# One buffer fewer in the weight pipeline of a fused four-layer kernel

## The chip, the cores and the metric

The kernel runs on one core of a Trainium2 chip. The metric is the time on the device in microseconds (us), lower is better. The kernel before takes 1076.88 us, the median of 3 runs (1076.03 to 1077.47).

A core has five engines that run side by side, each with its own queue of instructions in program order: PE (TensorE, the matrix multiplier), DVE (VectorE), ACT (ScalarE), POOL (GpSimd) and SP (SyncE, which here only issues DMAs). They wait for one another by semaphores.

## The reference

Four layers work on one sequence of 256 tokens with 1024 features, all in 32-bit floats. Cut to what matters:

```
x (1, 256, 1024)
layer 0: h = rms_norm(x); proj = h @ even_w_in            # 1024 x 5120
         q, k, v, z_a, u, z_b = split(proj)
         o_a = stick_breaking_attention(q, k, v) * silu(z_a)
         o_b = s5_mixer(u, ...) * silu(z_b)               # complex diagonal state space, then GLU
         x = x + concat(o_a, o_b) @ even_w_out            # 1536 x 1024
layer 1: h = rms_norm(x); proj = h @ odd_w_in             # gated linear attention
         x = x + (rms_norm(gla(q, k, v, gate)) * silu(z)) @ odd_w_out
layers 2 and 3 (w_in: 1024 x 11264):
         h = rmsnorm(x) * (1 + scale) + shift; proj = h @ w_in
         y_att = dilated_window_attention(...) * silu(za)
         y_ret = retention(...) * silu(zr)
         merged = sigmoid(ga) * (y_att @ w_proj_attn) + sigmoid(gr) * (y_ret @ w_proj_ret)
         x = x + gate * (merged @ w_out)
return rmsnorm(x, final_norm_w)
```

shift, scale and gate of layers 2 and 3 come from silu(c) @ w_ada + b_ada. Every weight matrix is used once, for all 256 tokens.

## The kernel before

**The weight pieces.** All weight matrices that meet the whole sequence are cut into 306 pieces (numbered 0 to 305 here, in the order of use): two blocks of 128 rows by up to 512 columns, 512 KB. Each large product is made of three products of numbers rounded to the format fp32r: a weight piece is split into a high part WH (the piece, rounded) and a low part WL (the piece minus WH), the activations likewise into HTh and HTl (or YTh and YTl), and PE adds high by high, low by high and high by low. So each piece passes four engines:

1. SP loads it into one of NRAW = 6 buffers RAW (`load` in `sync_program`, L2482). For piece n it first waits until DVE is done with piece n - 6, which had the buffer.
2. ACT makes WH (`hi`, L1046 through `copy`), in one of NHL = 4 buffers. It waits until the piece has landed and until PE has read piece n - 4.
3. DVE makes WL (`lo`, L1526), after ACT.
4. PE multiplies (`half`, L593 to L595 for kind N, L602, L604 and L605 for kind T, `split_half`, L631 to L633). It waits for LO, the mark of step 3. A piece has two halves, and a half is one step of the program's clock, `time`: piece n is used in steps 2n and 2n + 1. A half of kind N with 512 columns is 6 matmuls of 512 columns, a half of kind T is 12 matmuls of 256 columns.

**The order by hand.** Every engine runs a loop over `time`, and tables at the top of the program (AT_S5, AT_SB_..., AT_GLA, AT_ATT, AT_RET, ...) say at which step it does its share of the other work: attention scores, state-space tables, gates, turns of 128x128 blocks through PE, and so on. At the end of each odd step ACT and DVE do `hi` and `lo` of the piece that is AHEAD = 3 pieces further on, `hi((time + 1) // 2 + AHEAD)`. The place of such a call in an engine's queue is called a slot below. In the slot of step 2n - 7 stands piece n. All the other work of that and of earlier steps stands ahead of it in the queue.

**Where one layer gives way to the next** (`next_layer` on ACT and DVE, `open_layer` on PE), the sums of squares, the norm and the turned activations of the new layer must be made. Before them ACT and DVE handle pieces n0 + 1 to n0 + 3, where n0 is the layer's first piece (54, 90 and 198). The last three pieces of a layer ("close", kind C) and the first three of the next one are used token half by token half: first ti = 0 of all three, then ti = 1. So the second and third of them are wanted one and two steps after the first.

**At the start** pieces 0 to 3 are made ahead of the loops, and then comes the chain of small operations that makes the state-space tables of layer 0 (`s5_...`), with `s5_near` and the `head_turn` transposes of k and q (L556) on PE at steps 26 to 30.

**The memory.** `dynamic_dma_scratch_size=4096` sets the room for descriptors of the DMAs that POOL issues (L2404 to L2408, L2364 and others).

Of the kernel before, what the change touches and what calls it, by code (L numbers as in the profile page):

```python
# [14 lines left out]

P = 128
KP = 2
NRAW, NHL = 6, 4
AHEAD = 3
EPS = 1e-6  # L20
NEG = -1e30
MAGIC = 1597463007.0
# [105 lines left out]
def program(nc, t, out):  # L128
    ctx = ExitStack()
    with ctx:  # L130
# [273 lines left out]
        def raw_landed(n):  # L404
# [10 lines left out]
        pe, act, dve, pool = (Engine(e, sem(n)) for e, n in (  # L415
            (nc.tensor, "pe_step"), (nc.scalar, "act_step"), (nc.vector, "dve_step"), (nc.gpsimd, "pool_step")))
# [627 lines left out]
        def scalar_program():  # L1044
# [3 lines left out]
            def hi(n):  # L1048
                raw, wh, _ = w_in(n)
                act.wait_ge(*raw_landed(n))  # L1050
                if n >= NHL:
                    act.wait_ge(*read(n - NHL))
                copy(wh, raw).then_inc(*act.mark(HI, n))
# [34 lines left out]
            def square(l, ti, n):  # L1088

                if l < 2:  # L1090
                    act.wait_ge(*RES_V.of(l, ti, n))
                elif n == 1:
                    act.wait_ge(*RES_V.of(l, ti, "x", 1))
                else:
                    act.wait_ge(*RES_P.of(l, ti))
                i = 2 * n + ti
                nc.scalar.activation(TK[:, ti, n, :], X[:, ti, 512 * n:512 * n + 512], ACT.Square,
                                     accum_out=NSS[l + 1][:, i:i + 1]).then_inc(*act.mark(SUMSQ, l + 1, ti, n))

            def next_layer(l):  # L1100

                n0 = (0, 54, H0[0], H0[1])[l]
                square(l - 1, 0, 0)
                square(l - 1, 0, 1)
                hi(n0 + 1)
                square(l - 1, 1, 0)
                hi(n0 + 2)
                turned(l, 0, 0)
                square(l - 1, 1, 1)
                turned(l, 0, 1)  # L1110
                hi(n0 + 3)
                turned(l, 0, 2)
                turned(l, 0, 3)
                for r in range(4):
                    turned(l, 1, r)
# [257 lines left out]
            for q in range(2):  # L1373
# [1 line left out]
                    for r in range(2):  # L1375
                        turned(0, ti, 2 * q + r)
                hi(1 + q)
            hi(3)
            nc.scalar.activation(dt, co["log_dt"], ACT.Exp).then_inc(*act.mark(S5_A, "dt"))
            act.wait_ge(*S5_V.of("er"))  # L1380
            nc.scalar.activation(er, er, ACT.Exp).then_inc(*act.mark(S5_A, "er"))
# [1 line left out]
            for time in range(2 * groups["zr"]["at"] - 6):  # L1383
                if time in ENDS:
                    evac0(ENDS[time])
                if time == 1:
                    act.wait_ge(*S5_V.of("angle"))
                    nc.scalar.activation(tmp, th, ACT.Sin, scale=0.5).then_inc(*act.mark(S5_A, "half"))
                    nc.scalar.activation(sn, th, ACT.Sin).then_inc(*act.mark(S5_A, "sin"))
                if time in AT_SB_EXP:  # L1390
                    b, i = AT_SB_EXP[time]
                    act.wait_ge(*SB_W.of(b, 2 * i + 1))
                    z = flat(Z)[:, 768 * i:768 * i + 768]
                    nc.scalar.activation(z, z, ACT.Exp, scale=-1.0).then_inc(*act.mark(SB_EXP, b, i))
                if time in AT_HEAD_TURN:
                    key, c = AT_HEAD_TURN[time]
                    act.wait_ge(*side("ht", key, c))
                    if key == "k0":
                        act.wait_ge(*S5_V.of("im"))
                    dst, scale = (QT, gqs) if key[0] == "q" else (KT, co["sb_k_g"])  # L1400
                    if key[0] == "q":
                        act.wait_ge(*GQS.of("q"))
                    k = 4 * int(key[1]) + 2 * c
                    copy(dst[:, k:k + 2, :], pair(bank_of["ht", key, c]), scale=scale).then_inc(
                        *act.mark(HEAD_T, key, c))
                for b in range(2):
                    if 0 <= time - AT_SB_LN[b] < 6:
                        sb_log(b, time)
                    if time == AT_SB_VALUES[b]:
                        for ti in range(2):  # L1410
                            act.wait_ge(*side("sbo", b, ti))
                            copy(YB[b][:, ti, :], bank_of["sbo", b, ti][:, :]).then_inc(*act.mark(SB_O, b, ti))
                if time == AT_SB_VALUES[1]:
                    nc.scalar.activation(cact, co["c"], ACT.Tanh, scale=0.5).then_inc(*act.mark(CACT, "th"))
                for b, c in AT_SB_TURN.get(time, ()):
                    yt_hi(4 * b + c, "sb", b, c)
                if time in AT_S5["block"]:
                    s5_block(AT_S5["block"][time])
                if time in AT_S5["spread"]:
                    s5_spread(AT_S5["spread"].index(time))  # L1420
                if time in AT_S5["near_out"]:
                    s5_near(AT_S5["near_out"].index(time))
                if time in AT_S5["turn"]:
                    s5_turned(AT_S5["turn"].index(time))
                if time in AT_S5["out"]:
                    s5_y(AT_S5["out"].index(time))
                if time in AT_GELU.values():
                    gelu(time)
                if time in AT_GLU_OUT:
                    i = AT_GLU_OUT.index(time)  # L1430
                    act.wait_ge(*GLU_V.of(i))
                    act.wait_ge(*tile("glu", 1))
                    copy(YTh[:, 8 + 2 * i:10 + 2 * i, :], GY[:, 2 * i:2 * i + 2, :]).then_inc(
                        *act.mark(YT_HI, "glu", 2 * i))
                if time % 2:
                    hi((time + 1) // 2 + AHEAD)
# [83 lines left out]
        def vector_program():  # L1520
            vt, ts, stt = nc.vector.tensor_tensor, nc.vector.tensor_scalar, nc.vector.scalar_tensor_tensor

            def lo(n):
                raw, wh, wl = w_in(n)
                dve.wait_ge(*HI.of(n))
                vt(wl, raw, wh.bitcast(F32), ALU.subtract).then_inc(*dve.mark(LO, n))  # L1526
# [82 lines left out]
            def next_layer(l):  # L1609

                n0 = (0, 54, H0[0], H0[1])[l]
                residual(l - 1, 0, 0)
                residual(l - 1, 0, 1)
                residual(l - 1, 1, 0)
                rstd(l, 0)
                scaled(l, 0)
                residual(l - 1, 1, 1)
                lo(n0 + 1)
                turned(l, 0, 0)
                turned(l, 0, 1)  # L1620
                lo(n0 + 2)
                rstd(l, 1)
                scaled(l, 1)
                lo(n0 + 3)
                turned(l, 0, 2)
                turned(l, 0, 3)
                for r in range(4):
                    turned(l, 1, r)
# [504 lines left out]
            for q in range(2):  # L2133
# [1 line left out]
                    for r in range(2):  # L2135
                        turned(0, ti, 2 * q + r)
                lo(1 + q)
            lo(3)
            ts(gqs, co["sb_q_g"], 128.0 ** -0.5, None, ALU.mult).then_inc(*dve.mark(GQS, "q"))
            ts(gbh, co["s5_bg"], 0.5, None, ALU.mult).then_inc(*dve.mark(GB_V, "b"))  # L2140
            dve.wait_ge(*S5_A.of("dt"))
# [476 lines left out]
```

## Time and profile before

| | |
|---|---|
| median of 3 runs | 1076.88 us |
| the profiled execution | 1076.03 us |
| its span, first to last instruction | 1074.2 us |
| PE busy | 1021.6 us, 95% |
| DVE busy | 704.9 us, 66% |
| ACT busy | 565.3 us, 53% |
| POOL busy | 336.5 us, 31% |
| mean share of the 16 DMA engines, weight queue q1 | 49.6% |

Busy time is the union of an engine's instructions. PE's matmuls are pipelined, and a record ends only some tenths of a microsecond after the next one has started; the distance from start to start is what a matmul costs: 0.23 us for 512 columns, 0.12 us for 256. "Idle before, releaser" is the time for which the engine had nothing running ahead of an instruction, and what ended it. The views used below are the page of the profile, the waits (who waited for whom), the timeline (instructions in order of time, equal neighbours merged), and windows (busy time in chosen stretches, with the granted TensorE clock as a share of its full rate).

### The profile page before, as it was taken

Reading aid. Unit: us, or ns where it says so; the run is one execution under the profiler, and the core shown is the slowest. Engines: PE = TensorE matmul, PEld = TensorE weight load, DVE = VectorE, ACT = ScalarE, POOL = GpSimd, SP = SyncE. Lnnn points to the kernel's source line nnn. Section 1 sums busy time; section 2 is a strip of 40 time slices with the busy share of each in tenths; the row PEclk is TensorE's granted clock in tenths of the full one; section 3 lists DMA queues with packets and bytes.
Section 4 is the critical chain, followed back from the end, with each engine's and each line's share of the span. In section 5 each row is a group of like instructions: output and inputs, shape, how many; then the busy total and the mean of one; then the engine's idle time right before and its main releaser. Section 6 shows DMA issues by size and latency. Waiting matters only on the chain.

```text
span 1074.2 us, 15495 instructions
## 1 busy us (share of the span) xinstructions
PE 1021.6 (95%) x6084; PEld 900.2 (84%) x6084; DVE 704.9 (66%) x1072; ACT 565.3 (53%) x872; POOL 336.5 (31%) x349
## 2 busy tenths in 40 slices
PE   5999999989999799999999989979999999999995
PEld 5778889878968689998899868868999888998884
DVE  7894856888767664455576686774544565667665
ACT  5978577557344754455443344455444555334552
POOL 4700150433530173552453545321744000320001
PEclk9999999999999999999999989999999999999998
DMA  8543424767736487765565556745877436644531
GB/s 277 154 141 101 141 93 140 251 206 246 216 113 215 145 266 217 241 200 153 177 214 178 164 170 206 225 128 177 249 216 216 122 118 177 185 148 147 187 137 59
DMA packets 94440, 191.12 MB, mean 178 GB/s; under 512 B 6768, under 2 KB 10096, under 8 KB 94368
## 3 DMA queue, kind: packets, MB, share of 16 engines
q1 hardware_dynamic: 86256, 164.71, 49.6%
q0 software_dynamic: 6960, 22.71, 6.8%
q10 hardware_dynamic: 1152, 2.72, 0.7%
q8 instruction: 48, 0.79, 0.3%
q14 instruction: 24, 0.20, 0.1%
HBM read 189.07 MB, written 1.05 MB: 177 GB/s over the span
## 4 chain that ended last, share of the span: by engine, by line
PE 86%; DVE 6%; ACT 5%; DMA 1%; issue 1%; DVEq 0%; SPq 0%; ACTq 0%
PE G L593 15%; PE G L595 14%; PE G L594 14%; PE G L602 8%; PE G L604 8%; PE G L605 8%; PE B L556 2%; DVE WL L1526 1%; ACT AR L1046 1%; ACT WH L1046 1%; PE G L631 1%; PE G L633 1%; PE G L632 1%; DMA RAW<-in_even_w_in 1%; PE B L905 1%
## 5 line engine op out<-in xcount | busy, mean ns | idle before, releaser
L1526 DVE TENSOR_TENSOR WL<-RAW,WH 128x1024 fp32r<-128x1024 f32 (+2 forms) x306 | 398.5, 1306 | 258.2 <-ACT WH L1046 257.4
L1046 ACT ACTIVATE WH<-RAW 128x1024 fp32r<-128x1024 f32 (+2 forms) x306 | 320.2, 1050 | 282.9 <-PE G L595 142.7
L593 PE MATMUL G<-WH,HTh 128*128 128x512 f32 (+1 forms) x564 | 227.7, 404 | 2.8 <-DVE WL L1526 2.5
L602 PE MATMUL G<-HTh,WH 128*128 128x256 f32 x768 | 220.2, 287 | 0.5 <-DVE HTl L1602 0.5
L595 PE MATMUL G<-WL,HTh 128*128 128x512 f32 (+1 forms) x564 | 218.7, 388 | 0.0
L604 PE MATMUL G<-HTl,WH 128*128 128x256 f32 x768 | 217.9, 284 | 0.0
L605 PE MATMUL G<-HTh,WL 128*128 128x256 f32 x768 | 217.8, 284 | 0.0
L594 PE MATMUL G<-WH,HTl 128*128 128x512 f32 (+1 forms) x564 | 217.8, 386 | 0.0
L602 PEld LDWEIGHTS G<-HTh,WH 128*128 128x128 f32 x768 | 147.1, 191 | 2.4 <-issue 2.2
L604 PEld LDWEIGHTS G<-HTl,WH 128*128 128x128 f32 x768 | 147.1, 191 | 0.9 <-issue 0.7
L605 PEld LDWEIGHTS G<-HTh,WL 128*128 128x128 f32 x768 | 147.0, 191 | 0.0
L2364 POOL DMA_DIRECT2D AR<-in_w_ada x80 | 47.7, 596 | 278.6 <-PE G L595 160.0
L593 PEld LDWEIGHTS G<-WH,HTh 128*128 128x128 f32 x564 | 106.4, 189 | 24.1 <-DVE WL L1526 3.8
L595 PEld LDWEIGHTS G<-WL,HTh 128*128 128x128 f32 x564 | 106.1, 188 | 21.9
L594 PEld LDWEIGHTS G<-WH,HTl 128*128 128x128 f32 x564 | 106.6, 189 | 18.3 <-issue 0.2
L2380 POOL TENSOR_TENSOR AR<-AR 128x512 f32<-128x512 f32 x70 | 118.6, 1694 | 5.8
L593 PE MATMUL G<-WH,YTh 128*128 128x512 f32 x184 | 73.0, 397 | 0.0
L595 PE MATMUL G<-WL,YTh 128*128 128x512 f32 x184 | 71.8, 390 | 0.0
L594 PE MATMUL G<-WH,YTl 128*128 128x512 f32 x184 | 71.7, 389 | 0.0
L1046 ACT ACTIVATE AR<-B 128x512 f32<-128x512 f32 (+5 forms) x83 | 43.1, 547 | 45.3 <-PE B L950 22.4
L2378 POOL TENSOR_SCALAR AR<-AR,SM 128x512 f32<-128x512 f32 x70 | 59.2, 845 | 15.0 <-DMA AR<-in_w_ada 8.8
L2398 POOL TENSOR_TENSOR AR<-AR 128x256 f32<-128x256 f32 x16 | 18.2, 1141 | 139.8 <-DVE AR L2025 138.6
(344 smaller groups left out, 1343.9 us busy)
## 6 DMA issues: line engine op xcount, KB each, us to landing
RAW<-in_w_in SPq DMA_DIRECT2D x176, 512.0 KB, 3.8
RAW<-in_even_w_in SPq DMA_DIRECT2D x40, 512.0 KB, 3.7
AR<-in_w_ada POOLq DMA_DIRECT2D x80, 256.0 KB, 3.9
RAW<-in_odd_w_in SPq DMA_DIRECT2D x16, 512.0 KB, 4.9
RAW<-in_w_proj_ret SPq DMA_DIRECT2D x16, 512.0 KB, 3.5
RAW<-in_w_out SPq DMA_DIRECT2D x16, 512.0 KB, 4.2
RAW<-in_even_w_out SPq DMA_DIRECT2D x12, 512.0 KB, 3.9
AR<-in_w_ada SPq DMA_DIRECT2D x16, 256.0 KB, 4.3
```

What stands on the lines that cost most here:

```text
L556: ins = nc.tensor.transpose(ps[:, 128 * k:128 * k + 128], src(ti, j), IDENT)
L593: nc.tensor.matmul(o, xh, wh, start=begins, stop=False)
L594: nc.tensor.matmul(o, xl, wh, start=False, stop=False)
L595: ins = nc.tensor.matmul(o, xh, wl, start=False, stop=ends)
L602: nc.tensor.matmul(o, fh, h_[:, kx, :], start=begins and f % 2 == 0, stop=False, skip_group_check=True)
L604: nc.tensor.matmul(o, fh, l_[:, kx, :], start=False, stop=False, skip_group_check=True)
L605: ins = nc.tensor.matmul(o, fl, h_[:, kx, :], start=False, stop=ends and f % 2 == 1, skip_group_check=True)
L1046: return nc.scalar.activation(out_, ps, ACT.Copy, **kw)
L1526: vt(wl, raw, wh.bitcast(F32), ALU.subtract).then_inc(*dve.mark(LO, n))
L2364: nc.gpsimd.dma_start(dst, wv[:, k, 512 * cg:512 * cg + 512]).then_inc(s_ada[3 + i % 2], 16)
L2378: gts(w, w, cact[:, k:k + 1], 0.0, ALU.mult, ALU.add).then_inc(*pool.tick())
L2380: gtt(acc, acc, w, ALU.add).then_inc(*pool.mark(ADA_P, l, i))
```

## The change

Four numbers change: 5 instead of 6 buffers RAW, 3 instead of 4 buffers WH and WL, AHEAD 2 instead of 3, and the descriptor room goes back to the default. ACT then waits with `hi(n)` for PE to have read piece n - 3, and SP waits with `load(n)` for DVE to be done with piece n - 5. With AHEAD = 2 piece n stands in the slot of step 2n - 5.

```diff
-NRAW, NHL = 6, 4
-AHEAD = 3
+NRAW, NHL = 5, 3
+AHEAD = 2
...
 (next_layer on ACT)
                 square(l - 1, 0, 0)
                 square(l - 1, 0, 1)
+                hi(n0)
+                square(l - 1, 1, 0)
                 hi(n0 + 1)
-                square(l - 1, 1, 0)
-                hi(n0 + 2)
                 turned(l, 0, 0)
                 square(l - 1, 1, 1)
                 turned(l, 0, 1)
-                hi(n0 + 3)
+                hi(n0 + 2)
...
 (start of ACT)
                 hi(1 + q)
-            hi(3)
             nc.scalar.activation(dt, co["log_dt"], ACT.Exp).then_inc(*act.mark(S5_A, "dt"))
...
 (loop of ACT, layer 0)
                     act.wait_ge(*side("ht", key, c))
-                    if key == "k0":
-                        act.wait_ge(*S5_V.of("im"))
...
 (next_layer on DVE)
                 residual(l - 1, 1, 1)
-                lo(n0 + 1)
+                lo(n0)
                 turned(l, 0, 0)
                 turned(l, 0, 1)
-                lo(n0 + 2)
+                lo(n0 + 1)
                 rstd(l, 1)
                 scaled(l, 1)
-                lo(n0 + 3)
+                lo(n0 + 2)
...
 (start of DVE)
                 lo(1 + q)
-            lo(3)
...
-    nc = _bacc.Bacc("TRN2", target_bir_lowering=False, num_devices=1, dynamic_dma_scratch_size=4096)
+    nc = _bacc.Bacc("TRN2", target_bir_lowering=False, num_devices=1)
```

The order of the instructions on ACT at the start of the program, before the change. WH<-RAW is a `hi`; "waits rawK" names the buffer RAW of the piece, "stream" is a wait for PE to have read an earlier piece.

```order
L1046 ACTIVATE WH<-RAW 128x1024 [waits raw2]
L1046 ACTIVATE WH<-RAW 128x1024 [waits raw3]
L1379 ACTIVATE SM<-SM 128x16
L1381 ACTIVATE SM<-SM 128x16 [waits s5_v]
L1388 ACT_TABLE_LOAD
L1388 ACTIVATE SM<-SM 128x16 [waits s5_v]
L1389 ACTIVATE SM<-SM 128x16
L1046 ACTIVATE WH<-RAW 128x1024 [waits stream,raw4]
```

And after the change, at the same place:

```order
L1046 ACTIVATE WH<-RAW 128x1024 [waits raw2]
L1378 ACTIVATE SM<-SM 128x16
L1380 ACTIVATE SM<-SM 128x16 [waits s5_v]
L1387 ACT_TABLE_LOAD
L1387 ACTIVATE SM<-SM 128x16 [waits s5_v]
L1388 ACTIVATE SM<-SM 128x16
L1046 ACTIVATE WH<-RAW 128x1024 [waits stream,raw3]
```

The piece in RAW 3, piece 3, has moved behind the exponentials and sines of the tables, into the slot in which piece 4 stood.

ACT at steps 15 to 23 of layer 0, before. L1137 and TK<-G take q0 (first three rows) and then k0 (last row) out of PSUM, the YF rows are blocks of the state-space tables.

```order
L1137 ACTIVATE TK,SM<-G 128x128 [waits stream]
L1137 ACTIVATE TK,SM<-G 128x128 x3
L1046 ACTIVATE TK<-G 128x512 [waits act_step] x2
L1046 ACTIVATE WH<-RAW 128x1024 [waits raw5]
L1046 ACTIVATE WH<-RAW 128x1024 [waits stream,raw0]
L1046 ACTIVATE YF<-AR 64x16x16 [waits s5_v]
L1046 ACTIVATE YF<-AR 64x16x16 x3
L1046 ACTIVATE YF<-AR 64x3x16x16 [waits s5_v]
L1046 ACTIVATE YF<-AR 64x3x16x16
L1046 ACTIVATE WH<-RAW 128x1024 [waits stream,raw1]
L1046 ACTIVATE WH<-RAW 128x1024 [waits stream,raw2]
```

And after:

```order
L1137 ACTIVATE TK,SM<-G 128x128 [waits stream]
L1137 ACTIVATE TK,SM<-G 128x128 x3
L1046 ACTIVATE TK<-G 128x512 [waits act_step] x2
L1046 ACTIVATE WH<-RAW 128x1024 [waits raw0]
L1046 ACTIVATE WH<-RAW 128x1024 [waits stream,raw1]
L1046 ACTIVATE YF<-AR 64x16x16 [waits s5_v]
L1046 ACTIVATE YF<-AR 64x16x16 x3
L1046 ACTIVATE YF<-AR 64x3x16x16 [waits s5_v]
L1046 ACTIVATE YF<-AR 64x3x16x16
L1046 ACTIVATE WH<-RAW 128x1024 [waits stream,raw2]
L1046 ACTIVATE WH<-RAW 128x1024 [waits stream,raw3]
```

The slots stand where they stood, but what was piece 11 (11 mod 6 is RAW 5) is now piece 10 (10 mod 5 is RAW 0), and so on: from piece 3 on each slot holds the piece before the one that it held. DVE's queue is altered in the same way, and PE's is the same.

## Rows read from the trace of the kernel before

**Rows 1.** The page: span, busy us (share) xinstructions, and the granted clock.
```profile
span 1074.2 us, 15495 instructions
PE 1021.6 (95%) x6084; PEld 900.2 (84%) x6084; DVE 704.9 (66%) x1072; ACT 565.3 (53%) x872; POOL 336.5 (31%) x349
PEclk9999999999999999999999989999999999999998
```

**Rows 2.** The waits: engine line <- whom: us in total, times, longest.
```profile
DVE WL L1526 <- ACT WH L1046: 257.4, 180, 7.6
ACT WH L1046 <- PE G L595: 142.7, 93, 4.1
...
PE B L556 <- DVE AR L2105: 4.9, 1, 4.9
PE G L593 <- DVE WL L1526: 2.5, 1, 2.5
...
SPq L2482 <- DVE WL L1526: 892.4, 299, 9.7
```

**Rows 3.** A window of layer 3 (pieces of kind T).
```profile
core 0: us, PE busy (x) PEld busy (x) DVE busy (x) ACT busy (x) POOL busy (x), PEclk, DMA share, GB/s
757.00:803.00 46.00, 46.00 (x380) 45.52 (x379) 21.50 (x17) 20.59 (x23) 25.33 (x27) 1.00 0.75 231
```

**Rows 4.** Timeline there, ACT and DVE: start us, us, instruction [idle before <-releaser].
```profile
774.21 1.06 ACT L1046 ACTIVATE WH<-RAW 128x1024 fp32r<-128x1024 f32 x1 [1.82 <-PE G L605]
...
775.31 1.23 DVE L1526 TENSOR_TENSOR WL<-RAW,WH 128x1024 fp32r<-128x1024 f32 x1 [1.35 <-ACT WH L1046]
```

**Rows 5.** All WL: times, ns min/median/max, first and last start.
```profile
L1526 DVE TENSOR_TENSOR WL<-RAW,WH x306: 846/1226/2317, 13.4 to 1053.0; 128x1024 fp32r<-128x1024 f32 x147, 128x704 fp32r<-128x704 f32 x4, 128x672 fp32r<-128x672 f32 x2
```

**Rows 6.** Timeline of layer 0's start: DVE and PE.
```profile
19.90 2.34 DVE L1526 TENSOR_TENSOR WL<-RAW,WH 128x1024 fp32r<-128x1024 f32 x2
...
49.12 2.88 DVE L1526 TENSOR_TENSOR WL<-RAW,WH 128x1024 fp32r<-128x1024 f32 x2 [2.65 <-ACT WH L1046]
...
60.11 1.22 DVE L1526 TENSOR_TENSOR WL<-RAW,WH 128x1024 fp32r<-128x1024 f32 x1
...
50.92 0.50 PE L593 MATMUL G<-WH,HTh 128*128 128x512 f32 x1 [2.52 <-DVE WL L1526]
51.26 0.39 PE L594 MATMUL G<-WH,HTl 128*128 128x512 f32 x1
...
60.28 0.66 PE L556 MATMUL B<-CI,TK 128*128 128x128 f32 x4 [1.90 <-ACT TK L1046]
```

**Rows 7.** Windows behind it (columns as in rows 3).
```profile
80.00:120.00 40.00, 40.00 (x238) 35.05 (x237) 24.70 (x48) 29.75 (x69) 0.00 (x0) 1.00 0.39 113
```

**Rows 8.** Timeline of layer 0's end: DVE, then PE.
```profile
209.49 2.32 DVE L1526 TENSOR_TENSOR WL<-RAW,WH 128x1024 fp32r<-128x1024 f32 x1
...
215.17 3.45 DVE L1526 TENSOR_TENSOR WL<-RAW,WH 128x1024 fp32r<-128x1024 f32 x2
...
204.46 0.40 PE L593 MATMUL G<-WH,YTh 128*128 128x512 f32 x1
...
218.09 0.39 PE L631 MATMUL G<-WH,YTh 128*128 128x512 f32 x1
```

**Rows 9.** Timeline of layer 2's first pieces: DVE, then PE.
```profile
370.15 1.23 DVE L1526 TENSOR_TENSOR WL<-RAW,WH 128x1024 fp32r<-128x1024 f32 x1 [1.13 <-ACT WH L1046]
...
370.61 0.39 PE L593 MATMUL G<-WH,HTh 128*128 128x512 f32 x1
```

**Rows 10.** Timeline of layer 2's gates: DVE, then PE.
```profile
632.94 3.45 DVE L1526 TENSOR_TENSOR WL<-RAW,WH 128x1024 fp32r<-128x1024 f32 x2
...
631.24 0.39 PE L593 MATMUL G<-WH,YTh 128*128 128x512 f32 x1
...
639.00 1.97 PE L556 MATMUL B<-CI,AR 128*128 128x128 f32 x8 [4.87 <-DVE AR L2105]
```

**Rows 11.** Windows there (columns as in rows 3).
```profile
633.00:637.00 4.00, 1.12 (x5) 0.58 (x4) 4.00 (x6) 0.00 (x0) 1.17 (x1) 0.98 0.14 37
637.00:644.00 7.00, 5.00 (x19) 4.32 (x20) 6.97 (x12) 2.62 (x5) 0.00 (x0) 0.52 0.64 208
```

**Rows 12.** The page's DMA issues: out<-in xcount, KB each, us to landing.
```profile
RAW<-in_w_in SPq DMA_DIRECT2D x176, 512.0 KB, 3.8
AR<-in_w_ada POOLq DMA_DIRECT2D x80, 256.0 KB, 3.9
```

## The prediction, made before the changed kernel was run

> **What bounds the kernel now.** I read the page first: PE is busy for 1021.6 of 1074.2 us, at its higher clock of 2.4 GHz in nearly all slices, while DVE has 66% and ACT 53% [rows 1]. So the kernel is as long as PE's work plus PE's waits, and a change in the weight pipeline counts only where PE waits longer or less. The waits say how it stands: ACT waits for PE and DVE for ACT, for hundreds of microseconds, and SP waits 299 times for DVE, which is a full pipeline; PE itself waited for a WL just once, 2.5 us [rows 2]. Then I went through the timeline slot by slot.
>
> In steady state a piece of kind T is 24 matmuls, and 380 of them take 46 us [rows 3], so a piece takes 2.9 us (kind N: 12 by 0.227 us, 2.7 us). ACT starts WH of a piece as soon as PE has read the piece four before it (774.21), and DVE is done with WL at 775.31 + 1.23 = 776.54, 2.4 us after PE's release [rows 4]. PE comes to that piece three pieces after the release: 8.7 us. The spare time is 6.3 us.
>
> **The rule of the change.** All slots stay where they are in the queues of ACT and DVE, and the slot that waits for PE to have read piece m waits for the same m: before it was piece n of n - 4, now it holds piece n - 1, which waits for (n - 1) - 3. So until PE is held up, everything on ACT and DVE happens when it happened before, but each WL comes for the piece that PE wants one piece sooner. The test is then simple: where WL of piece n + 1 ended after PE's first matmul of piece n, there is a new wait, as long as the difference. In steady state 6.3 - 2.9 = 3.4 us stay spare (kind N: 3.0), and nothing is lost. I made the test for all 306 pieces; it fails only where other work on DVE or ACT is bunched.
>
> **Term 1, layer 0's tables: +2.5 us.** ACT is held by taking q0 out of PSUM, and its two slots behind that end late; of DVE's pair at 49.12 the first ends at about 50.87, when PE starts piece 11 at 50.92 after 2.52 us of waiting [rows 6]. Now the same slot holds piece 10, which PE wants at 50.92 - 2.52 - 2.72 = 45.7. It waits 5.2 us, but that isn't the cost. Pieces 10, 11 and 12 then run from 50.9 to 59.1, and piece 13 needs the slot that ends at 60.11 + 1.22 = 61.33 [rows 6] and runs its first half to 62.75. The head transposes behind that half started at 60.28, since they waited for ACT [rows 6]. PE is late by 2.5 us, and as it is busy without a gap from 80 to 120 us [rows 7], it stays so. Bounds: 0, if the tables come earlier by more than I allow; 5.2, if the whole wait is paid. I take 2.5, which goes by the rows.
>
> The dropped `hi(3)` and `lo(3)` put the tables' chain forward by half of 2.34 us [rows 6]. I count nothing: ACT then comes to the copy of u out of PSUM, which waits for PE's piece 3. Without that cover it is worth -1.2.
>
> **Term 2, the end of layer 0: +2.2 us.** PE runs five pieces from 204.46 to 218.09 [rows 8], so 48 starts at 209.9 and 50 at 215.4. WL in the slot now for 48 ends at 209.49 + 2.32 = 211.81: 1.9 late. The pair at 215.17 has its first end at 217.5 (the second takes 1.2): for piece 50 that is 2.1 after 215.4, of which 1.9 is already paid. Together 2.2 with the semaphore. No wait behind it is long enough to take it back, as the residual sums that follow wait for PE. Bounds 0 and 3.8 (1.9 and 1.9 apart).
>
> **Term 3, the starts of layers 1, 2 and 3: +0.8 us at most each, 2.1 together.** ACT may make WH of the fourth piece only when PE has read the first. At layer 2, WL of the slot ends at 370.15 + 1.23 = 371.38, and PE wanted its fourth piece, 93, at 370.61 [rows 9]: 0.8. The same reckoning gives 0.7 at layer 1 and 0.55 at layer 3. Bounds 0 and 1.4 each (a half piece).
>
> **Term 4, the first pieces of layer 1's output: +0.4 us**, by the same test at pieces 80 to 82. Bounds 0 and 1.
>
> **Restarts: +0.6 us.** After a wait the second matmul comes 0.34 us after the first (50.92, 51.26) and not 0.23 [rows 6]; six waits by 0.1.
>
> **Layer 2's gates: 0.** PE wanted piece 173 at 631.24; the slot now for it is the first of the pair at 632.94, which ends near 635.2: a new wait of 4 us. But PE stood still from 634.1 to 639.0 for DVE L2105 [rows 10], a chain that doesn't hang on this piece. Now it does the piece from 635.3 to 638.0 and waits for the same event 1 us. Bounds: -2.4 and +1.7, from the clock: before, the clock fell to 1.2 GHz for the 7 us that began inside this pause (0.52 granted from 637 to 644) [rows 11]; a broken pause may leave it alone, or the fall may come earlier and catch piece 173.
>
> The Trainium skill bears on this ("TensorE: Matmul & The Clock Gate", Part 1): an idle PE goes back to its lower clock. Here the trace agrees, by the fall after the pause of 4.87 us [rows 10, 11], and the pause of 2.52 us at 48.4 was not followed by one. By that rule term 1's new pause of 5 us puts pieces 10 to 12 at the lower clock; they have 61.33 - 50.9 = 10.4 us for 8.2, and a stretch as long as that of rows 11 would cost 2.3, so it is just covered.
>
> **SP and POOL: 0.** A load is asked for five pieces ahead instead of six, 14 us, and takes 3.8 to land [rows 12]; SP waits for buffers nearly always [rows 2]. The smallest distance between a landing and ACT's start becomes 2.8 us, at the start of layer 2. The descriptor room changes nothing that POOL was seen to wait for; bounds -1 and +1. The dropped wait of the first k turn was over by 60.2, when DVE's table was done, before PE's turn: 0. At the very end one more WL (1.2 us) stands ahead of the last residual; it is hidden by ACT's next square, which waits for other sums.
>
> **Sum.** 2.5 + 2.2 + 2.1 + 0.4 + 0.6 = 7.8. The profiled execution took 1076.03 us, so 1083.8; it was the fastest of the three, 0.85 below the median, so the forecast for the median is 1084.6 us. Its own range is 1080.5 to 1088.5.
>
> **Rivals.** (a) 3 us of spare time are not enough in steady state. For: WL takes up to 2.3 us instead of 1.2 [rows 5], and 27 pieces have less than 2 us left by my test. If a quarter of these lose 0.8 more, it is 1090. Against: most of those are near the places already counted. The Trainium skill ("Perfetto Trace Analysis", Optimization Strategy) says that a gap that repeats on the engine that should be full can mean too few buffers; such gaps would be this rival's sign, the trace of before has none, and by rows 3 and 4 I expect none. (b) The late times are taken back: term 1 by the earlier tables and term 2 by shorter WL, so that only 2 us are left: 1078.8, no change that can be told. Against: PE has no gap after term 1 [rows 7]. (c) Faster: the pause at 634 to 639 was one long pause, and its low clock cost 2.4 us; broken in two it costs nothing, and the tables start 1.2 earlier. That is 1076.9 - 3.6 = 1073.3 if the new waits stay away, and it decides only if they add less than 1.5 us; I see 7. (d) The clock: new pauses bring low stretches at terms 1 and 2 that are not covered, 2 to 4 us more: 1087 to 1088. (e) The change doesn't do what it says, if the buffers never filled: excluded by ACT's waits [rows 2]; it would be 1077.
>
> **How the numbers follow.** Forecast 62%, (a) 13%, (b) 13%, (c) 3%, (d) 7%, (e) 2%. A measurement of this kernel can tell 0.2%, 2.15 us. Faster by more: (c), and little of (b): 0.04. Same: most of (b), (e): 0.12. Slower: 0.84. The range runs from 1078.5, the edge of (b), to 1091, which holds (a) and (d).
>
> **What would show it.** Waits of PE for WL: seven or eight instead of one, near 46 (5 us), 61, 210, 215, 240, 371, 632 and 733, together about 15 us, with the wait for L2105 down from 4.9 to about 1. PE's piece 14 starts 2.5 us later, the first residual of layer 0 about 4.7 later, the end 7 to 8 later. Wrong if PE waits for WL in the middle of the T stretches, or if ACT's WH waits for a landing.

## The result and the profile after

The changed kernel takes 1083.12 us, the median of 4 runs (1082.04 to 1083.72), the kernel before 1077.18 us in the same comparison. The ratio is 1.0057 with a 95% interval of 1.0045 to 1.0068: slower by 5.9 us. The forecast was 1084.6 us, in a range of 1078.5 to 1091.

The page of the changed kernel, against [rows 1]:

```profile
span 1080.6 us, 15495 instructions
PE 1023.9 (95%) x6084; PEld 899.1 (83%) x6084; DVE 703.8 (65%) x1072; ACT 565.1 (52%) x872; POOL 339.1 (31%) x349
PEclk9899999999999999999999999999999999999997
```

The number of instructions is the same; PE's busy time grew by 2.3 us, the span by 6.4. The waits of the changed kernel, PE's rows, against [rows 2]:

```profile
PE G L593 <- DVE WL L1523: 10.9, 6, 3.8
...
PE G L631 <- DVE WL L1523: 1.2, 1, 1.2
...
PE B L556 <- DVE AR L2102: 0.2, 1, 0.2
```

PE waits for a WL seven times instead of once, 12.1 us in all, and hardly for the gate (L2102 was L2105 and L1523 was L1526 before). The timeline shows the first of these waits, at piece 10 (DVE, then PE), against [rows 6]:

```profile
48.40 2.42 DVE L1523 TENSOR_TENSOR WL<-RAW,WH 128x1024 fp32r<-128x1024 f32 x2 [2.80 <-ACT WH L1046]
...
49.74 0.79 PE L593 MATMUL G<-WH,HTh 128*128 128x512 f32 x1 [3.77 <-DVE WL L1523]
```

Piece 48, against [rows 8]: DVE's glu and modulation products stand ahead of the slot, as before, and PE now wants the WL 1.75 us before it is there.

```profile
209.68 1.43 DVE L1698 SCALAR_TENSOR_TENSOR AR<-AR 128x512 f32<-128x512 f32 x1
211.02 2.30 DVE L1523 TENSOR_TENSOR WL<-RAW,WH 128x1024 fp32r<-128x1024 f32 x1
...
213.38 0.50 PE L593 MATMUL G<-WH,YTh 128*128 128x512 f32 x1 [1.75 <-DVE WL L1523]
```

The start of layer 2, against [rows 9], and layer 2's gates, against [rows 10]:

```profile
364.06 0.50 PE L631 MATMUL G<-WH,HTh 128*128 128x512 f32 x1 [1.17 <-DVE WL L1523]
...
377.36 0.50 PE L593 MATMUL G<-WH,HTh 128*128 128x512 f32 x1 [0.90 <-DVE WL L1523]
...
641.07 0.50 PE L593 MATMUL G<-WH,YTh 128*128 128x512 f32 x1 [2.74 <-DVE WL L1523]
...
645.85 1.09 PE L556 MATMUL B<-CI,AR 128*128 128x128 f32 x8 [0.22 <-DVE AR L2102]
```

The wait of 4.87 us for the gate has become one of 2.74 for WL and one of 0.22. The windows there, against [rows 11] (the third begins with the gate's arrival at 645.8):

```profile
637.00:644.00 7.00, 4.26 (x15) 3.09 (x14) 6.97 (x9) 1.24 (x2) 4.52 (x3) 0.87 0.50 171
642.00:646.00 4.00, 3.78 (x11) 2.42 (x10) 3.97 (x7) 0.00 (x0) 0.15 (x1) 0.57 0.71 245
645.80:652.00 6.20, 6.15 (x35) 5.33 (x36) 6.20 (x12) 5.04 (x10) 0.00 (x0) 1.00 0.30 110
```

The low clock is half as long as before, some 3.5 us and not 7. What counts more is where it lies. In the kernel before, the gate came at 639.0 and the 4.7 us of PE's work behind it ran at half the clock:

```profile
639.00:643.70 4.70, 4.70 (x16) 4.01 (x17) 4.70 (x8) 2.62 (x5) 0.00 (x0) 0.50 0.67 205
```

In the changed kernel the low clock falls on piece 173, ahead of the gate, where PE would have stood waiting for the gate in any case, and behind the gate PE works at the full clock.

**The ledger.** Both programs run the same 4800 matmuls into the banks G in the same order, so the start of the same matmul can be compared in the two traces. The changed kernel's last one starts 3.75 us later than before. The span grew by 6.4. The rest is at the very end, in the closing instructions of the program, the rows of line L130: each engine ends with a DRAIN, and then the engines wait for one another. GpSimd and SP are shown. The columns are the duration in ns (least, median, most) and the first and last start in us. The kernel before:

```profile
L130 POOLq DRAIN  x1: 3009/3009/3009, 1068.3 to 1068.3; - x1
L130 SPq DRAIN  x1: 7/7/7, 1074.0 to 1074.0; - x1
L130 SPq EVENT_SEMAPHORE  x1: 17/17/17, 1074.1 to 1074.1; - x1
```

And the changed kernel:

```profile
L130 POOLq DRAIN  x1: 8562/8562/8562, 1071.8 to 1071.8; - x1
L130 SPq DRAIN  x1: 7/7/7, 1077.5 to 1077.5; - x1
L130 SPq EVENT_SEMAPHORE  x1: 17/17/17, 1080.5 to 1080.5; - x1
```

Before, SP's wait for the output ends last (1074.0), and GpSimd's DRAIN had been done since 1071.3. After, SP is done at 1077.5 and everybody waits for a DRAIN of 8.56 us, which ends at 1080.4: 2.9 us that no instruction of the kernel fills.

### The profile page after: what moved, and what is told of

It reads as the page before. It is cut to its first block, busy times and chain, and to the rows that moved or that the text cites. A ratio compares the mean times of both kernels' runs of the same rounds, so it can differ in the third digit from the quotient of the medians.

```text
span 1080.6 us, 15495 instructions
## 1 busy us (share of the span) xinstructions
PE 1023.9 (95%) x6084; PEld 899.1 (83%) x6084; DVE 703.8 (65%) x1072; ACT 565.1 (52%) x872; POOL 339.1 (31%) x349
## 3 DMA queue, kind: packets, MB, share of 16 engines
q10 hardware_dynamic: 1152, 2.72, 0.7%
## 4 chain that ended last, share of the span: by engine, by line
PE 86%; DVE 7%; ACT 4%; DMA 1%; issue 1%; DVEq 0%; SPq 0%; ACTq 0%
PE G L593 15%; PE G L595 14%; PE G L594 14%; PE G L602 8%; PE G L604 8%; PE G L605 8%; DVE WL L1523 2%; PE B L556 2%; ACT AR L1046 1%; ACT WH L1046 1%; DMA RAW<-in_even_w_in 1%; PE G L631 1%; PE G L633 1%; PE G L632 1%; PE B L905 1%
## 5 line engine op out<-in xcount | busy, mean ns | idle before, releaser
L1523 DVE TENSOR_TENSOR WL<-RAW,WH 128x1024 fp32r<-128x1024 f32 (+2 forms) x306 | 396.4, 1298 | 266.8 <-ACT WH L1046 265.9
L602 PE MATMUL G<-HTh,WH 128*128 128x256 f32 x768 | 219.9, 286 | 0.5 <-DVE HTl L1599 0.5
L602 PEld LDWEIGHTS G<-HTh,WH 128*128 128x128 f32 x768 | 146.8, 191 | 2.4 <-issue 2.2
L2374 POOL TENSOR_SCALAR AR<-AR,SM 128x512 f32<-128x512 f32 x70 | 62.0, 886 | 19.5 <-DMA AR<-in_w_ada 13.9
```

The costliest lines, as they stand in the source:

```text
L602: nc.tensor.matmul(o, fh, h_[:, kx, :], start=begins and f % 2 == 0, stop=False, skip_group_check=True)
L2374: gts(w, w, cact[:, k:k + 1], 0.0, ALU.mult, ALU.add).then_inc(*pool.tick())
```

## Experiments

### The parts of the change one by one

Four kernels, beside a kernel before of 1077.10 us.

The changed kernel with the small descriptor room:

```diff
-    nc = _bacc.Bacc("TRN2", target_bir_lowering=False, num_devices=1)
+    nc = _bacc.Bacc("TRN2", target_bir_lowering=False, num_devices=1, dynamic_dma_scratch_size=4096)
```

> The changed kernel with the descriptor room back at 4096 (5 RAW, 3 WH and WL, AHEAD 2 stay). Theory D: the 5.9 us have two parts. PE's waits cost about 3.5 (its last piece ends 3.75 later), and the room costs 2.9 at the very end, since GpSimd's closing DRAIN took 8.56 us in the changed kernel and 3.01 before, and ends 2.9 us after SP's last event. Then this run is 2.9 below the changed kernel: 1080.2, 3.0 above before; DRAIN 3.0. Rival P: all of it is in the weight pipeline, the DRAIN's length is chance: 1083.1.

Measured: 1080.42 us, ratio 1.0029 (1.0019 to 1.0038). The DRAIN is back at 3.0 us:

```profile
L130 POOLq DRAIN  x1: 3007/3007/3007, 1072.8 to 1072.8; - x1
L130 SPq DRAIN  x1: 7/7/7, 1078.5 to 1078.5; - x1
```

Theory D holds: 2.7 us of the loss are the descriptor room, 3.3 the pipeline. In the profiled execution PE's last matmul is no earlier than in the changed kernel, so the 2.7 us came from behind it.

The kernel before with one RAW buffer fewer:

```diff
-NRAW, NHL = 6, 4
+NRAW, NHL = 5, 4
```

> The kernel before with 5 RAW buffers instead of 6, nothing else. Theory: loads are far enough ahead, 0 +- 0.5: 1077.2. Rival L: the loads carry part of the loss: 1078.5 to 1080, and ACT's WH waits for landings.

Measured: 1076.85 us, ratio 0.9992 (0.9977 to 1.0008). The sixth buffer is worth nothing that this interval (-2.5 to +0.9 us) would show.

The same with twice the room:

```diff
-NRAW, NHL = 6, 4
+NRAW, NHL = 5, 4
...
-    nc = _bacc.Bacc("TRN2", target_bir_lowering=False, num_devices=1, dynamic_dma_scratch_size=4096)
+    nc = _bacc.Bacc("TRN2", target_bir_lowering=False, num_devices=1, dynamic_dma_scratch_size=8192)
```

> The kernel before with 5 RAW buffers and a descriptor room of 8192. Theory D with a DRAIN in proportion to the room: without the 1.26 us of work inside it the DRAIN is 1.75 at 4096 and 7.3 at 16384, so 3.6 at 8192, 4.9 with the work; it ends before SP's last event, so the time is that of 5 RAW alone, 1077.2. Rival P: DRAIN 3.0 or 8.6. Rival: every byte of room costs time elsewhere (PE steps other than 5 RAW alone): 1078.2 or more.

Measured: 1077.17 us, ratio 1.0007 (0.9992 to 1.0022). The time is as expected, the DRAIN isn't: it is as short as at 4096, so its length is not in proportion to the room.

```profile
L130 POOLq DRAIN  x1: 2927/2927/2927, 1071.2 to 1071.2; - x1
```

Three WH and WL and AHEAD 2 alone, with 6 RAW and the small room (beside a_room4096):

```diff
-NRAW, NHL = 5, 3
+NRAW, NHL = 6, 3
```

> The kernel before with 3 instead of 4 WH and WL, AHEAD 2 and the moved calls, but 6 RAW and a room of 4096. Theory: all of PE's new waits come from this part, so it equals the changed kernel with a room of 4096, 1080.2 within 0.5. Rival L: the sixth RAW buffer gives back 1 us or more.

Measured: 1080.10 us, ratio 1.0038 (1.0019 to 1.0057), the same as with 5 RAW. The pipeline's loss goes with three instead of four WH and WL, with AHEAD 2 and with the moved calls, and not with RAW. No run separates these three.

### How long the DRAIN is at 12288

The changed kernel with a room between 8192 and the default:

```diff
-    nc = _bacc.Bacc("TRN2", target_bir_lowering=False, num_devices=1)
+    nc = _bacc.Bacc("TRN2", target_bir_lowering=False, num_devices=1, dynamic_dma_scratch_size=12288)
```

> The changed kernel with a descriptor room of 12288. GpSimd's closing DRAIN took 3.01, 2.93 and 8.56 us at 4096, 8192 and 16384, so it isn't in proportion. Theory T1: it jumps between 8192 and 12288 (8 to 9 us, and 1083 as in the changed kernel). Theory T2: only the full 16384 is slow: DRAIN 3, 1080.4. A value between (5 to 6) hides behind the output's transfer: 1080.4.

Measured: 1083.47 us (2 runs), ratio 1.0066 (1.0042 to 1.0091). T1 holds: the DRAIN jumps between 8192 and 12288, and SP is done 2.7 us before it. (8192 was measured on the four-buffer kernel, 12288 on the changed one; at 4096 both have 3.0 us.)

```profile
L130 POOLq DRAIN  x1: 8399/8399/8399, 1074.0 to 1074.0; - x1
L130 SPq DRAIN  x1: 7/7/7, 1079.7 to 1079.7; - x1
```

What the DRAIN does in these 5.4 us more the trace doesn't say, and it stays open.

### Undoing terms 1 and 2

Both edits are made in the changed kernel with the room of 4096. First, WH of piece 10 before the copies out of PSUM:

```diff
+                if time == 15:
+                    hi(10)
                 if time in ENDS:
                     evac0(ENDS[time])
...
-                if time % 2:
+                if time % 2 and time != 15:
                     hi((time + 1) // 2 + AHEAD)
```

> The changed kernel with a room of 4096 (1080.4 in a_room4096), and in step 15 ACT makes WH of piece 10 before it takes q0 and k0 out of PSUM, not after. It undoes term 1. WL of piece 10 can then start when DVE is free, at about 45.6, and ends near 46.9 where PE wants it at 46.0, so the wait of 3.7 us falls to about 1 and piece 13 is no longer late. Theory: term 1 is worth its 2.2 to 2.5 us: 1078.1. Rival (b): the late time is taken back by what follows (PE's transposes wait for k0, now 1.1 later): 1079.5 to 1080.4.

Measured: 1079.05 us, ratio 1.0019 (1.0006 to 1.0032). The interval overlaps that of a_room4096, so the times alone don't decide between the two. The trace does: the wait of 3.7 us before piece 10 has turned into four, 4.9 us in all.

```profile
46.82 0.50 PE L593 MATMUL G<-WH,HTh 128*128 128x512 f32 x1 [0.85 <-DVE WL L1525]
50.62 0.50 PE L593 MATMUL G<-WH,HTh 128*128 128x512 f32 x1 [0.78 <-DVE WL L1525]
55.38 0.47 PE L593 MATMUL G<-WH,HTh 128*128 128x512 f32 x1 [1.74 <-DVE WL L1525]
59.96 0.50 PE L593 MATMUL G<-WH,HTh 128*128 128x512 f32 x1 [1.57 <-DVE WL L1525]
```

At piece 40 PE is 1.1 us later than in the kernel before, and 1.5, 2.1 and 2.3 in the three kernels with this change of the pipeline (table below): a gain of 0.4 to 1.1, where 2.3 had been expected. So term 1 is no matter of one slot: the slot of piece 13 stands behind DVE's table work, as the prediction's term 1 has it, and as long as that is there, PE is late by it. My expectation of 1078.1 was too good, for it looked at the slot of piece 10 alone.

Then, DVE's modulation products later:

```diff
-AT_ADA0 = (82, 86, 90, 94, 98, 112, 116, 120) + tuple(130 + 4 * i for i in range(8))
+AT_ADA0 = (82, 86, 92, 96, 100, 112, 116, 120) + tuple(130 + 4 * i for i in range(8))
```

> The changed kernel with a room of 4096, and DVE's third, fourth and fifth modulation products (L1918) two steps later, at 92, 96 and 100 instead of 90, 94 and 98. It undoes term 2: 1.8 us of DVE work ahead of WL of piece 48 goes behind it. Theory: the gap of 1.75 before piece 48 goes and nothing comes in its place, 1078.5. Rival (b): term 2 had been taken back by later pauses, 1080.4. Rival: the work meets the slots of 49 and 50 instead, 1079.5.

Measured: 1079.59 us, ratio 1.0031 (1.0021 to 1.0041), no gain that the times show. The gap before piece 48 fell from 1.75 to 0.35 us, but the moved products now stand ahead of the next slots, as the third theory said, and a YTl of 1.78 us with them, which took 0.68 in a_room4096; in a_ada GpSimd was adding beside it for 1.2 us, in a_room4096 not. DVE in a_ada:

```profile
212.10 1.22 DVE L1523 TENSOR_TENSOR WL<-RAW,WH 128x1024 fp32r<-128x1024 f32 x1
213.24 0.74 DVE L1918 SCALAR_TENSOR_TENSOR AR<-AR,SM 128x512 f32<-128x512 f32 x1
...
216.14 1.78 DVE L2190 TENSOR_TENSOR YTl<-AR,YTh 128x512 fp32r<-128x512 f32 x1
217.84 1.21 DVE L1523 TENSOR_TENSOR WL<-RAW,WH 128x1024 fp32r<-128x1024 f32 x1
```

WL of piece 50 ends at 217.84 + 1.21 = 219.05; PE, which began piece 48 at 213.37, wants it at 213.37 + 2 x 2.72 = 218.81. From piece 40 to 52 PE still loses 1.7 us in small waits like this (0.35 before piece 48, 0.44 before piece 53), where a_room4096 loses 2.1. As in a_head, taking one piece of work away from one slot isn't enough where DVE is full over several.

### The spare time in steady state

Ten pieces of kind T in undisturbed stretches get extra work on DVE: WL is made k times more, k being 4 or 2, with the same result. a_dve4 and a_dve2 are the changed kernel with the room of 4096, b_dve4 is the kernel before.

```diff
+                if n in (107, 111, 115, 119, 154, 158, 215, 219, 223, 227):
+                    for _ in range(k):
+                        vt(wl, raw, wh.bitcast(F32), ALU.subtract).then_inc(*dve.tick())
+                        dve.wait_ge(*dve.prev)
                 vt(wl, raw, wh.bitcast(F32), ALU.subtract).then_inc(*dve.mark(LO, n))
```

> The changed kernel with a room of 4096 (1080.4), and at ten pieces in undisturbed stretches (107, 111, 115, 119, 154, 158, 215, 219, 223, 227) DVE makes WL five times over, 4 x 1.2 to 1.3 = 5 us of extra work in one slot. It measures the steady-state spare time. Theory: WL ended 2.9 to 3.4 us ahead of PE there, so each place costs 5.0 - 3.3 = 1.7 and 0.1 for the restart: ten new waits of PE for WL, 1.6 to 2.2 us each, 18 together: 1098. Rival (a) (the spare time is smaller than the slots say): more than 25.

> The kernel before with the 5 us of extra work at the same ten pieces. Theory: there WL ended 5.6 to 6.2 us ahead of PE, so nothing: 1077.1 within 1. Rival: any DVE work in these stretches costs PE time, 1080 or more.

> The same with WL made three times over, 2.5 us of extra work. Theory: less than 2.9, so nothing: 1080.4 within 1, and no new wait of PE at the ten pieces. Rival (a): waits of 0.5 or more at the ten places, 1085.

Measured, beside a kernel before of 1075.85: a_dve4 1129.41 us, ratio 1.0500 (1.0478 to 1.0522); b_dve4 1088.18, ratio 1.0109 (1.0090 to 1.0128); a_dve2 1082.76, ratio 1.0063 (1.0046 to 1.0080). All three are above what I expected, and the traces say why. The four extra subtractions took 5.0 us where GpSimd was idle and up to 8.0 where it was busy for most of the time. In a_dve4, at pieces 115 and 154:

```profile
446.35 7.60 DVE L1525 TENSOR_TENSOR WL<-RAW,WH 128x1024 fp32r<-128x1024 f32 x4 [2.31 <-ACT WH L1046]
...
592.55 5.01 DVE L1525 TENSOR_TENSOR WL<-RAW,WH 128x1024 fp32r<-128x1024 f32 x4 [2.45 <-ACT WH L1046]
```

And windows in the two places (the fifth time is GpSimd's):

```profile
446.40:453.90 7.50, 4.24 (x36) 4.03 (x34) 7.40 (x4) 3.21 (x4) 5.69 (x5) 0.91 0.34 107
594.00:600.00 6.00, 4.15 (x32) 3.98 (x32) 5.90 (x6) 2.12 (x2) 0.00 (x0) 0.95 0.06 9
```

Four subtractions take 7.60 us with GpSimd busy for 5.69 of them, and 5.01 with it idle. The windows differ in their DMA traffic too, but that isn't it: in a_dve2 the two extra subtractions of piece 158 took 2.5 us at a DMA share of 0.80, with GpSimd idle. Nor does every instruction of GpSimd do it: at piece 115 of a_dve2 GpSimd was busy for half of the time with a DMA issue and a TENSOR_SCALAR, and the extra work still took 2.5. Which of GpSimd's instructions stretch DVE's, no run separates.

With the real length the theory fits. The extra work, measured from the first extra subtraction to the start of the last one, minus PE's wait is the spare time. In a_dve4 the ten places give 5.84 - 2.56 = 3.3 (piece 107), 7.63 - 4.62 = 3.0 (115), 5.04 - 1.85 = 3.2 (154 and 158), and so on: 2.3 to 3.3, the middle one 3.1. In b_dve4 seven of the ten places have a wait, and they give 5.2 to 6.2, the middle one 5.6 (7.46 - 2.22 at piece 115):

```profile
PE G L602 <- DVE WL L1530: 10.1, 7, 2.2
```

The fourth buffer is worth 2.5 us, nearly a piece. In a_dve2 the extra work was hidden at seven of ten places, where it took 2.5 to 2.8 us; where it took 2.9 to 3.8, three waits of 0.2 to 0.6 us came. In b_dve4 the waits are 10.1 us of the 12.3. So rival (a) is wrong about the spare time and right that GpSimd eats into it.

And a wait costs more than its length. In a_dve4 the waits for WL are 32.5 us over the ten places:

```profile
PE G L602 <- DVE WL L1527: 32.5, 10, 4.6
```

Yet PE is 48.6 us later at the end than in a_room4096, and 48.0 of it arose over the ten places. A part of the difference lies in how a wait is counted: the view counts it from the end of the last record, which here is 0.16 us after the next matmul would have started, and the restart adds 0.1, so ten waits cost 2.6 us more than the view has. The rest, some 13 us, is the clock. A window behind the wait at piece 111, and the next one:

```profile
436.00:442.50 6.50, 6.36 (x30) 6.37 (x31) 2.85 (x3) 0.78 (x1) 3.85 (x3) 0.51 0.81 256
442.50:449.00 6.50, 6.50 (x56) 6.50 (x56) 3.84 (x3) 3.15 (x5) 3.45 (x3) 1.00 0.50 152
```

At 0.51 of the full clock PE does 30 matmuls where it then does 56. Seven new stretches like this come with the ten waits, 34 us together by the granted clock. About 4 of the 34 lie inside the waits, where they cost nothing; of the other 30, by the two windows, somewhat under half is lost, 13 to 14 us: 32.5 + 2.6 + 13.5 = 48.6, for the 48.0 found. The Trainium skill ("TensorE: Matmul & The Clock Gate", Part 1) counts half of the time at the low clock as lost. That would be 15 us of these 30 (an estimate by its rule), and the trace agrees roughly, with 13 found.

### What the fourth buffer is good for

In the kernel before PE stands still at the gates of layer 2 until DVE is through with them and with the WL between them, and in the changed kernel it waits there for a WL. The turns on PE that wait for the gate need not stand so early; their results are wanted only at step 176.

```diff
-          "turn": {167: (0, 2), 168: (4, 6)}}
+          "turn": {170: (0, 2), 172: (4, 6)}}
```

> The kernel before, with the turns of the gated retention output on PE, ACT and DVE two and four half pieces later, steps 170 and 172 of a layer instead of 167 and 168. In layer 2 PE's 4.87 us of waiting for the gate then lie beside pieces 174 and 175, of which the first WL comes 1.2 late. Theory: 3.7 us less waiting, and another 2.4 if the low clock of 6.8 us behind the pause goes with it: 1071. Rival: the WL of pieces 175 to 177, held up by the same DVE work, take the pause's place: 1074 to 1077.

> The same move of the turns in the changed kernel with a room of 4096 (1080.4). Theory: here PE waits for WL of piece 173 (2.7 to 3.4 us) and hardly for the gate (0.2 in one profile, 1.8 in another), and with three buffers the WL of 174 comes 2.4 us ahead of PE, not more: gain 0 to 1, 1080.0; the fourth buffer is what lets the move pay in the kernel before. Rival: it gains as much as there, 1075.

Measured: b_turn 1069.85 us, ratio 0.9935 (0.9923 to 0.9947), the fastest kernel of this study; a_turn 1080.43, ratio 1.0036 (1.0023 to 1.0049), no gain at all. Both as expected. In b_turn the pause of 4.87 us is 0.37, and no low clock follows it (the granted clock is full from 368 to 719 us):

```profile
639.90 1.09 PE L556 MATMUL B<-CI,AR 128*128 128x128 f32 x8 [0.37 <-DVE AR L2105]
```

With three buffers PE has to wait for WL of piece 173 whatever the turns do, 3.42 us in a_turn; with four it has pieces 173 to 175 to do while DVE finishes the gate.

## Why the prediction was right, step by step

How late PE is against the kernel before, in us, by the start of the same matmul (52, 88 and 196 are pieces of a layer's close, in their second half; the last row is the last matmul):

| at piece | after | a_room4096 | a_raw6_room4096 | b_raw5 | b_turn |
|---|---|---|---|---|---|
| 2 | -0.66 | -0.30 | -0.23 | -1.04 | -1.33 |
| 40 | 1.54 | 2.15 | 2.28 | 0.49 | -0.32 |
| 52 | 3.63 | 4.24 | 4.36 | 0.49 | -0.32 |
| 70 | 5.26 | 5.84 | 5.95 | 0.49 | 0.94 |
| 88 | 5.68 | 6.24 | 6.38 | 0.51 | 0.98 |
| 110 | 6.92 | 7.25 | 7.36 | 0.47 | 0.95 |
| 171 | 6.92 | 7.25 | 7.36 | 0.62 | 0.95 |
| 180 | 4.65 | 5.68 | 5.09 | 0.57 | -4.98 |
| 196 | 4.69 | 5.75 | 5.15 | 0.58 | -4.96 |
| 210 | 3.72 | 4.78 | 4.22 | 0.51 | -5.91 |
| 305 | 3.75 | 4.80 | 4.26 | 0.50 | -6.19 |

The direction was right, and so was the mechanism: every slot holds the piece before, and PE waits only where other work is bunched. The size, 7.8 forecast and 5.9 measured, came out near by luck, because two errors of opposite sign met: the pipeline cost 3.3 us (a_room4096), less than half of the 7.8, and the descriptor room, counted as nothing, cost 2.7.

- **Term 1, +2.5:** at piece 40 PE is 1.5 us late in the changed kernel and 2.1 and 2.3 in the other two. The mechanism was right, the size somewhat high. Counted from piece 2 it is 2.2, 2.45 and 2.5, but not all of that belongs to the change: b_turn and b_raw5, with four buffers, lose 1.0 and 1.5 on the same way. They were ahead at piece 2, since PE's slow first stretch ended sooner (the windows from 16.4 to 19.1 us hold 13 matmuls in the kernel before, 18 in the changed one, 24 in b_turn), and they gave the lead back at piece 11, where PE waits for WL with four buffers too (2.5 us before, 3.6 and 3.7 in these). The low clock behind the new pause (0.50 from 48.3 to 55.1) was just covered, as forecast: PE had no gap before piece 13. But that the old pause left the clock alone is true of the one profile of the kernel before that the forecast had; the four other four-buffer profiles have a low stretch of some 3.5 or 7 us there.
- **Term 2, +2.2:** 2.1 in all three. Right. It was all paid at piece 48 (the wait and the restart behind it); piece 50 added nothing.
- **Term 3, +2.1 for three starts:** 1.6, 1.2 and -1.0, together 1.9. The sum came out right by luck, for its parts are wrong. At layer 1 the forecast wait of 0.7 for a WL did not come: PE waits for none there. b_turn loses 1.3 as well, with no buffer changed, and a_ada, with three buffers, only 0.4; so most of that step is where the low clock falls. At layer 2 the step is 0.9 us of waiting at piece 93 as forecast (0.8); the wait of 1.17 us for WL of piece 91 wasn't, and cost nothing, since the pause that follows it shrank from 2.05 to 0.99. At layer 3 the new wait was 1.25 us, for a forecast of 0.55, and it was paid, but more than 2 came back: before, 7 us of low clock lay on the matmuls of its first pieces; after, the low clock came at the first matmuls, ahead of a pause, and the pause took it up. The two windows, of before and of after:

```profile
722.00:729.00 7.00, 5.69 (x19) 4.43 (x17) 2.87 (x6) 3.86 (x11) 1.24 (x1) 0.51 0.26 77
```

```profile
720.70:724.20 3.50, 2.92 (x7) 2.30 (x8) 2.43 (x8) 3.44 (x10) 0.00 (x0) 0.51 0.47 150
```

And the pause of the changed kernel, in PE's timeline:

```profile
726.37 0.66 PE L694 MATMUL B<-CI,TK 128*128 128x128 f32 x4 [0.76 <-DVE TK L1588]
```

Before, this pause was 2.04 us long and lay ahead of the low stretch. With four buffers b_turn gets 0.95 back here too, and b_dve4, whose low stretch also came ahead of the pause, 2.5, so it is a matter of the clock and not of the change.
- **Term 4, +0.4:** from piece 70 to 88, 0.42, 0.40 and 0.43. Right; it comes in steps of 0.15 us and less at pieces 80, 81 and 83.
- **Restarts, +0.6:** the second matmul after the new waits comes 0.34 us after the first, as forecast (641.07 and 641.41 at piece 173). In the table this is part of each step, so the terms above hold it already.
- **Layer 2's gates, 0:** -2.3, -1.6 and -2.3. This is a term that was mis-sized. I had written the bound of -2.4 and its reason, that a broken pause may leave the clock alone, and then took 0. The gate itself came no sooner for PE: PE starts on it 6.85 us later than before (645.85 and 639.00), about as late as it was ahead of the pause (6.92). The gain is all behind it, where the kernel before had 4.7 us of low clock and the changed kernel has none; half of 4.7 is 2.35. In a_raw6_room4096 there was no low clock there at all, and the gain is the same. In a_room4096 the low clock held piece 173 up until PE was 0.8 us late for the gate (646.13, and PE's turn at 646.93), and the gain is 1.6.
- **Descriptor room, 0 with bounds of 1:** +2.7 by a_room4096. This is the step that failed. "The descriptor room changes nothing that POOL was seen to wait for" is true of the queue and not of the end of the program: the DRAIN behind the last instruction was in the trace, 3.0 us long and hidden by 2.7 us, and I had neither read nor bounded it.
- **SP, the sixth RAW buffer, 0:** b_raw5 confirms it, and a_raw6_room4096 from the other side.
- **The spare time in steady state,** against rival (a): a_dve4 gives 3.1 us for a forecast of 3.4 (kind T), b_dve4 5.6 for 6.3; a_dve2 shows that 2.5 are hidden unless GpSimd stretches them. PE has no wait for a WL in the T stretches of the changed kernel. The sign by which the Trainium skill ("Perfetto Trace Analysis", Optimization Strategy) knows too few buffers, a gap that repeats on the engine that should be full, is there where work was added (at L602 ten times in a_dve4, seven in b_dve4, three in a_dve2) and not in the changed kernel: three buffers are enough for this steady state, and short only where work is bunched.
- **Rival (b),** late times taken back: not seen; what terms 1 and 2 cost is still there at piece 88.
- **Rival (c),** faster by the gates' clock and the earlier tables: its gain at the gates came (2.3 of the 2.4), and it lost to the new waits, as the text had it.
- **Rival (d),** uncovered low stretches at terms 1 and 2: none in the changed kernel's profile. In a_ada, a_room12288 and a_dve4 a second low stretch near 67 us makes PE 2.9 to 3.6 late at piece 40, but b_raw5_room8192, with four buffers, has it too (2.8).
- **The signs:** seven waits for WL were seen of the seven or eight named, but not all where they were named: near 46, 210, 371, 632 and 733 they came, later by what PE was late by then; at 61, 215 and 240 none did, and those of 0.5 us at piece 7 and 1.17 at piece 91 weren't named. Together they are 12.1 us, for about 15. ACT's WH waited for a landing once, 4.4 us at the start of the program, as before (4.3).

By the terms as measured the changed kernel's PE is late by 2.2 + 2.1 + 1.9 + 0.4 - 2.3 = 4.3, less the 0.66 by which it was ahead at piece 2: 3.6 of the 3.75. The final load of the norm's weights was 0.26 us quicker (3.37, before 3.63), and the DRAIN added 2.9: the span's 6.4.

## What to carry to other kernels

When a pipeline loses a buffer and keeps its slots, test each piece: where the next piece's operand came later than PE wanted this one, there is the new wait, and elsewhere nothing. The depth itself is worth one piece of spare time, which matters only where another engine's work is bunched. Before adding up such waits, look at which long pauses they break and where the low clock then falls: low clock ahead of a pause that comes anyway cost nothing here, and behind it 2.3 us, as much as a term. And read the last rows of the program, behind the last instruction of the kernel, for every engine, when an option of the build is changed.

## What the runs showed of the hardware

- GpSimd's closing DRAIN takes 3.0 us with a descriptor room of 4096 and 2.9 with 8192, but 8.4 with 12288 and 8.6 with the default (about 1.3 of it beside GpSimd's last addition). It sets the end of the program once it outlasts the output's transfer.
- In a_dve4 seven of PE's ten waits, of 1.8 to 4.6 us, came with stretches at 1.2 GHz, which cost some 13 us on top of 32.5 us of waiting; the three others (2.56, 1.85 and 1.76 us) didn't, nor did the wait of 1.75 us before piece 48 of the changed kernel. Where such a stretch falls changes from one profile to the next, and it moved single steps of the ledger by 1 to 2.5 us.
- A 128x1024 subtraction on DVE takes 1.25 us with GpSimd idle (5.01 us for four) and 1.9 us with GpSimd busy three quarters of the time (7.60 us for four).
